# A decoder layer with 32 experts on one core: last two experts' up projections ahead of their down ones, layer norm by channel blocks, parts of block 1 during the first gather, one MB of w_down loaded elsewhere

## The reference

```python
conv_o = silu(layernorm(conv(a * sigmoid(g)) + b_dw, ln_g, ln_b))
h = h + concat([att_o, conv_o]) @ w_out
hn = rmsnorm(h, norm_ffn_g)
gates = top4_softmax(hn @ w_router + b_router)       # (256, 32)
for e in range(32):                                  # w_gu[e]: 1024x2048, w_down[e]: 1024x1024
    hg, hu = split(hn @ w_gu[e] + b_gu[e])
    hg = minimum(hg, 7.0); hu = clip(hu, -7.0, 7.0)
    act = (hu + 1.0) * (hg * sigmoid(1.702 * hg))
    h = h + gates[:, e:e+1] * (act @ w_down[e] + b_down[e])
return rmsnorm(h, norm_final_g)
```

## Time and profile before

| | us |
|---|---|
| median of 3 runs | 1064.13 |
| lowest and highest | 1063.89, 1065.67 |
| the profiled execution | 1063.36 |
| its span in the trace | 1061.6 |
| TensorE busy | 994.2 (94%) |
| VectorE, ScalarE busy | 237.9 (22%), 138.9 (13%) |
| transfers | 421.49 MB, mean 397 GB/s |

### The profile page before, as it was taken

One profiled execution on the slowest core, in us unless ns is written; L12 is line 12 of the kernel. 1 busy time (PEld: TensorE's weight loads), 2 busy tenths in 40 slices (PEclk: granted clock), 3 DMA queues, 4 the chain that ended last, 5 costly groups with the idle time before them and its releaser, 6 DMA issues.

```text
span 1061.6 us, 12949 instructions
## 1 busy us (share of the span) xinstructions
PE 994.2 (94%) x5808; PEld 412.4 (39%) x5809; DVE 237.9 (22%) x531; ACT 138.9 (13%) x264; POOL 14.0 (1%) x27
## 2 busy tenths in 40 slices
PE   9998999999999999999999999999899999889996
PEld 7874443433333333333333333332333333333332
DVE  3995341111111111111111111100111111110113
ACT  4144220101010101010101000100101010100003
POOL 4000000000000000000000000000000000000000
PEclk9999999999999999999999999999999999999999
DMA  9984469999999999999999999999999999999993
GB/s 322 410 357 158 159 254 403 429 427 429 425 429 426 427 427 428 427 428 427 427 428 427 427 426 430 427 428 427 428 427 427 428 427 427 427 428 426 428 427 142
DMA packets 39241, 421.49 MB, mean 397 GB/s; under 512 B 5153, under 2 KB 9297, under 8 KB 14480
## 3 DMA queue, kind: packets, MB, share of 16 engines
q1 hardware_dynamic: 37376, 420.31, 94.5%
q10 hardware_dynamic: 1808, 0.33, 0.2%
HBM read 419.56 MB, written 1.05 MB: 396 GB/s over the span
## 4 chain that ended last, share of the span: by engine, by line
PE 53%; DMA 31%; DVE 12%; ACT 3%; issue 1%; ACTq 0%; DVEq 0%; POOL 0%; POOLq 0%
PE work L965 46%; DMA ring<-in_w_gu 31%; PE resid L965 5%; DVE main L716 4%; DVE main L902 2%; DVE main L899 2%; DVE main L895 2%; PE work L1282 2%; ACT main L585 1%; PE work L1080 0%; PE work L980 0%; ACT ring L528 0%; PE work L1174 0%; DVE main L958 0%; DVE ring L760 0%
## 5 line engine op out<-in xcount | busy, mean ns | idle before, releaser
L965 PE MATMUL work<-ring,main 128*64 128x512 f32 (+1 forms) x3104 | 686.7, 592 | 27.4 <-DMA ring<-in_w_gu 25.1
L965 PEld LDWEIGHTS work<-ring,main 128*64 128x64 f32 (+1 forms) x3104 | 222.8, 138 | 478.1 <-issue 422.2
L895 DVE TENSOR_SCALAR main<-work 128x512 f32<-128x512 f32 x32 | 22.1, 692 | 752.0 <-PE work L965 752.0
L585 ACT ACTIVATE main<-main 128x512 f32<-128x512 f32 x32 | 20.2, 631 | 501.9 <-DVE main L895 501.9
L965 PE MATMUL resid<-main 128*128 128x512 f32 x136 | 71.0, 612 | 0.9 <-DVE main L949 0.9
L965 PE MATMUL work<-ring 128*128 128x256 f32 (+2 forms) x304 | 71.1, 403 | 0.0
L596 ACT ACTIVATE main<-work 64x512 f32<-64x512 f32 x63 | 37.3, 592 | 227.6 <-PE work L965 227.3
L965 PE MATMUL work<-bgu_rows,ident 128*64 128x512 f32 x256 | 62.0, 605 | 0.0
L965 PEld LDWEIGHTS work<-ring 128*128 128x128 f32 (+1 forms) x304 | 54.9, 186 | 13.9 <-issue 6.2
L965 PEld LDWEIGHTS work<-select,main 128*128 128x128 bf16 x1584 | 48.0, 98 | 27.0 <-issue 27.0
L965 PE MATMUL work<-select,main 128*128 128x64 bf16 x1584 | 51.9, 193 | 0.9 <-DVE select L880 0.9
(11 more groups left out here) (178 smaller groups left out, 245.6 us busy)
## 6 DMA issues: line engine op xcount, KB each, us to landing
ring<-in_w_gu SPq DMA_DIRECT2D x128, 2048.0 KB, 40.4
ring<-in_w_down SPq DMA_DIRECT2D x63, 2048.0 KB, 41.3
ring<-in_w_in SPq DMA_DIRECT2D x3, 2048.0 KB, 14.8
ring<-in_w_in SPq DMA_DIRECT2D x4, 1024.0 KB, 12.2
ring<-in_w_out SPq DMA_DIRECT2D x2, 2048.0 KB, 19.5
ring<-in_w_down SPq DMA_DIRECT2D x2, 1024.0 KB, 6.0
main<-in_x SPq DMA_DIRECT2D x2, 512.0 KB, 4.1
result<-main SPq DMA_DIRECT2D x4, 256.0 KB, 2.3
```

Of the source, the lines that this page charges most:

```text
L585: nc.scalar.activation(sig_h, gate_h, ACT.Sigmoid, scale=SWIGLU_ALPHA).then_inc(sig_ready, 1)
L895: V.tensor_scalar(gate_h, work[:, GATE_BANK, :], SWIGLU_LIMIT, None, ALU.min).then_inc(gate_clamped, 1)
L965: return nc.tensor.matmul(out_, lhsT, rhs, start=start, stop=stop, skip_group_check=True)
```

## The change

- `SEQUENCE` sets the order of issue and use: experts 0 to 29 as before, then the up chunks of experts 30 and 31 (180 to 187), then their down chunks (188 to 191). The very last chunk is issued as two halves of 1 MB. TensorE runs expert 31's up projection ahead of expert 30's down projection.
- Layer norm: two additions in pairs in place of the strided sum of squares; each of four channel blocks is scaled by gain and 1/sigma in one operation and has its sigmoid behind it; copy_turned(0) stands ahead of the second products; conv_ready counts blocks, and TensorE's first projection waits for two of four.
- Block 1's parts: one of three operations stays ahead of the choice, one stands behind chosen_b, two third parts behind the first selection. gather_first runs over the parts in its outer loop, and its last of six waits for them. The two warm-up products go; expert 0's bias is split around the place products. turn_gates goes behind expert 3's down projection, b_down is loaded behind expert 2 and used in expert 4 on 32 partitions, with no clearing on GpSimd.
- Chunk 11: its rows 0 and 1 (512 KB each) go to a buffer of their own and to blocks 12 and 13, issued behind chunks 7 and 10; the second half goes to slot 0 as before.
- Final norm: products with the gain by halves ahead of the scale, then scaling; the last half is scaled by ScalarE.
- Some constants (mean_w, dw_cols, others, gates_t) move into other buffers.

```diff
+    SEQUENCE = [(e, i) for e in range(E - 2) for i in range(CHUNKS)]
+    SEQUENCE += [(e, i) for e in (E - 2, E - 1) for i in range(UP_CHUNKS)]
+    SEQUENCE += [(e, i) for e in (E - 2, E - 1) for i in range(UP_CHUNKS, CHUNKS)]
...
+    NUMBER = {chunk_: n for n, chunk_ in enumerate(SEQUENCE)}
...
+    def ups_used(e):
+        return NUMBER[e, UP_CHUNKS - 1] + 1
...
-        return (CHUNKS * e + i) % SLOTS
+        return NUMBER[e, i] % SLOTS
...
+                        CONV_SLOT: ((proj_done, 11), (conv_ready, CB)),
+                        KEYS_SLOT: ((tap_done, CB * OPS), (decay_in, 32), (scores_done, len(GROUPS))),
...
+                src = w_down[e, f:f + 4 * P, :].rearrange("(p h b) n -> p h (b n)", h=2, b=2)
+                to = chunk(slot_of(e, i)).rearrange("p (h n) -> p h n", h=2)
+                sp.dma_start(to[:, 0, :], src[:, 0, :]).then_inc(slot_full[slot_of(e, i)], 16)
+                sp.dma_start(to[:, 1, :], src[:, 1, :]).then_inc(last_half_in, 16)
...
+                sp.dma_start(spare_rows[b], rows_reused()[:, b, :]).then_inc(spare_in, 16)
...
+                sp.wait_ge(first_unit_used, 1)
+                sp.dma_start(unit(0).rearrange("p (b n) -> p b n", b=2), rows_reused()[:, 2:4, :]).then_inc(slot_full[0], 16)
...
+            for number, (e, i) in enumerate(SEQUENCE[:CHUNKS * E]):
+                if number == SLOTS:
+                    load_first_reused()
+                    continue
+                if number >= SLOTS:
+                    sp.wait_ge(slots_used, number - SLOTS + 1)
+                elif number in released:
+                    for used in released[number]:
+                        sp.wait_ge(*used)
+                if (e, i) == (E - 1, CHUNKS - 1):
+                    load_last_in_halves(e, i)
+                else:
                     load_chunk(e, i, slot_of(e, i))
+                if number in (CONV_SLOT, SLOTS - 1):
+                    load_spare_row(0 if number == CONV_SLOT else 1)
...
+                if n == HALVES - 1:
+                    sp.wait_ge(last_ready, 1)
...
-            pool.wait_ge(h_done, 3)
-            nc.gpsimd.memset(bdown_sb, 0.0).then_inc(moe_zeroed, 1)
-            pool.wait_ge(logits_done, TB)
-            nc.gpsimd.memset(gates_t, 0.0).then_inc(moe_zeroed, 1)
...
-            act.wait_ge(normed, 1)
             for c in range(CB):
-                done = nc.scalar.activation(ln_tmp[:, c, :], conv_y[:, c, :], ACT.Sigmoid,
-                                            scale=cols[:, LN_G + c:LN_G + c + 1], bias=cols[:, LN_B + c:LN_B + c + 1])
-            done.then_inc(swish_sig, 1)
+                act.wait_ge(normed, c + 1)
+                nc.scalar.activation(ln_tmp[:, c, :], conv_y[:, c, :], ACT.Sigmoid,
+                                     bias=cols[:, LN_B + c:LN_B + c + 1]).then_inc(swish_sig, 1)
...
+                act.wait_ge(gates_turned, 1)
+                nc.scalar.activation(gates_t, work[0:E, TURN_BANK, 0:SEQ], ACT.Copy).then_inc(gates_t_ready, 1)
...
+                act.wait_ge(slots_used, SLOTS + 1)
+                act.dma_start(bdown_sb, b_down).then_inc(bdown_in, 16)
...
-                if e > 0:
-                    copy_results(e - 1, (e - 1) // 2 % 2, (e - 1) % 2)
-                expert_pass(e)
+                if 0 < e < E - 1:
+                    copy_results(downs_used(e - 1), (e - 1) // 2 % 2, (e - 1) % 2)
+                gate_sigmoid(e)
+                if e < E - 1:
+                    copy_act(e)
                 if e % 2 == 1:
                     copy_scatter(pair, pair % 2, P, (pair - 1) * HALVES if pair > 1 else None)
+                if e == E - 1:
+                    copy_results(downs_used(e - 1), (e - 1) // 2 % 2, (e - 1) % 2)
+                    copy_act(e)
...
             for e in range(E):
                 expert(e)
+                if e == 2:
+                    load_bdown()
+                if e == BDOWN_EXPERT - 1:
+                    copy_gates()
...
+                if t == TB - 1:
+                    act.wait_ge(o_scale, TB)
+                    act.wait_ge(o_gained, HALVES)
+                    nc.scalar.activation(result[:, t, HALF:D], result[:, t, HALF:D], ACT.Copy, scale=stat[:, 10 + t:11 + t])\
+                        .then_inc(last_ready, 1)
...
-            V.tensor_reduce(channel_sum, ln_tmp.rearrange("p c t -> p t c"), AX.X, ALU.add).then_inc(squares_summed, 1)
+            V.tensor_tensor(ln_tmp[:, 0:2, :], ln_tmp[:, 0:2, :], ln_tmp[:, 2:4, :], ALU.add).then_inc(squares_paired, 1)
+            dve.wait_ge(squares_paired, 1)
+            V.tensor_tensor(channel_sum, ln_tmp[:, 0, :], ln_tmp[:, 1, :], ALU.add).then_inc(squares_summed, 1)
...
-            V.tensor_tensor(conv_y, conv_y, ln_s[:, 0, :].unsqueeze(1).to_broadcast([P, CB, SEQ]), ALU.mult)\
-                .then_inc(normed, 1)
             for c in range(CB):
-                if c == 0:
-                    dve.wait_ge(normed, 1)
-                    dve.wait_ge(swish_sig, 1)
-                V.tensor_scalar(conv_y[:, c, :], conv_y[:, c, :], cols[:, LN_G + c:LN_G + c + 1],
-                                cols[:, LN_B + c:LN_B + c + 1], ALU.mult, ALU.add).then_inc(ln_step, 1)
-            dve.wait_ge(ln_step, 1 + CB)
-            V.tensor_tensor(conv_y, conv_y, ln_tmp, ALU.mult).then_inc(conv_ready, 1)
+                V.scalar_tensor_tensor(conv_y[:, c, :], conv_y[:, c, :], cols[:, LN_G + c:LN_G + c + 1], ln_s[:, 0, :],
+                                       ALU.mult, ALU.mult).then_inc(normed, 1)
             copy_turned(0)
+            for c in range(CB):
+                dve.wait_ge(swish_sig, c + 1)
+                V.scalar_tensor_tensor(conv_y[:, c, :], conv_y[:, c, :], cols[:, LN_B + c:LN_B + c + 1], ln_tmp[:, c, :],
+                                       ALU.add, ALU.mult).then_inc(conv_ready, 1)
...
-                third_part(1, halves[1], 6)
+                less_first_part(1, halves[1], 4)
...
-            less_first_part(1, halves[1], 4)
-            third_part(1, halves[0], 5)
             choose()
...
             select_tokens(0, 0, 0)
+            third_part(1, halves[0], 5)
+            third_part(1, halves[1], 6)
             copy_tokens(0)
...
+                half = slice(h * HALF, (h + 1) * HALF)
+                dve.wait_ge(o_squared, 2 * t + h + 1)
+                V.tensor_tensor(result[:, t, half], resid[:, t, half], final_gain[:, half], ALU.mult).then_inc(o_gained, 1)
...
-                inv_rms_of_halves(t, 2 * t, stat[:, 2 * t:2 * t + 1], stat[:, 2 * t + 1:2 * t + 2], stat[:, 4 + t:5 + t],
-                                  (stat[:, 6 + t:7 + t], stat[:, 8 + t:9 + t]), stat[:, 10 + t:11 + t],
-                                  o_squared, o_mean, o_root, o_scale, roots_before=1)
-                for h in range(2):
+                gained(t, 0)
+                V.tensor_scalar(stat[:, 4 + t:5 + t], stat[:, 2 * t:2 * t + 1], 1.0 / D, RMS_EPS, ALU.mult, ALU.add).then_inc(o_mean, 1)
+                dve.wait_ge(o_mean, 2 * t + 1)
+                dve.wait_ge(o_squared, 2 * t + 2)
+                V.tensor_scalar(stat[:, 6 + t:7 + t], stat[:, 2 * t + 1:2 * t + 2], 1.0 / D, stat[:, 4 + t:5 + t], ALU.mult, ALU.add)\
+                    .then_inc(o_mean, 1)
+                gained(t, 1)
+                dve.wait_ge(o_root, t + 2)
+                V.reciprocal(stat[:, 10 + t:11 + t], stat[:, 8 + t:9 + t]).then_inc(o_scale, 1)
+                dve.wait_ge(o_scale, t + 1)
+                for h in range(TB - t):
                     half = slice(h * HALF, (h + 1) * HALF)
-                    V.scalar_tensor_tensor(result[:, t, half], resid[:, t, half], stat[:, 10 + t:11 + t], final_gain[:, half],
-                                           ALU.mult, ALU.mult).then_inc(result_ready, 1)
+                    dve.wait_ge(o_gained, 2 * t + h + 1)
+                    V.tensor_scalar(result[:, t, half], result[:, t, half], stat[:, 10 + t:11 + t], None, ALU.mult).then_inc(result_ready, 1)
...
-            pe.wait_ge(conv_ready, 1)
             arrived("out_conv")
+            pe.wait_ge(conv_ready, 2)
             project("out_conv", 0, 0, range(0, 2))
+            pe.wait_ge(conv_ready, CB)
...
-            keep_warm(2, work[:, GATE_BANK, 0:P])
-            bias(0)
+            bias(0, (GATE_BANK,))
...
+            bias(0, (UP_BANK,))
...
-                    if is_first and kb == KB // 2:
-                        turn_gates()
...
+                    reused = isinstance(n, int) and n == SLOTS // CHUNKS and UP_CHUNKS + m == SLOTS % CHUNKS
+                    if reused:
+                        pe.wait_ge(spare_in, 32)
...
+                        if is_last and f == FB - 2:
+                            pe.wait_ge(last_half_in, 16)
                         lhsT = act_t[:, f % 4, (f // 4) * CAP:(f // 4 + 1) * CAP]
+                        row = w[:, b * D:(b + 1) * D]
+                        if reused:
```

(43 more changed lines are left out.)

111 lines of the change are left out of this document (57 added, 54 removed).

## The result

The changed kernel takes 1057.34 us (median of 4 executions, 1056.44 to 1058.07), the kernel before 1064.90 in the same session (4, 1063.89 to 1065.69): ratio 0.9926, 95% interval 0.9911 to 0.9941. That is 7.6 us less, where 9.4 were forecast. The time lies in the range, and 2.6 above the forecast. The profiled execution took 1057.29, with a span of 1055.6: 6.0 less span than before.

What follows compares the result with a forecast made beforehand. It took the late-starting weight stream as the bound: end = issue of chunk 15 + 176 landings + what follows. Terms summed to -9.4 us from 1063.36, giving 1053.96, forecast as a 1054.7 median; range 1051.5 to 1059.5.

Steps and rivals of the forecast that it cites:

- a: Layer norm by blocks: TensorE's wait for the copy goes, first projection 4.6 us earlier (3.3 to 5.0).
- Rival 4: Layer norm: another wait replaces the copy's, only 1 or 2 of 4.6 us arrive, 1058; chance 0.07.
- b: Choice and first gather: earlier choice and split bias gain 1.1 us, between about 0 and 1.9 depending on clock.
- rival 1: Clock stays at 0.50 through first gather: that stage gains 0, perhaps layer norm 1.3 less; 1055.8 to 1057.1; chance 0.16.
- c: Gate transposes moved from expert 0 to behind expert 3's down projection: 0.4 us less before chunk 15's release.
- d: One MB of chunk 11 issued early: less queue ahead of chunks 12 to 15, gain 1.0 us (0 to 1.9).
- Rival 2: Transfer stream: the early MB pays its full 2.45 us, giving 1053.2; chance 0.10.
- e: b_down's 128 KB moves from the idle stretch into the weight stream: 0.3 us later.
- Rival 5: Weight stream: pace slows with more small rows; if the extra per chunk triples, +13.8 us, 1068.5; chance 0.05.
- f: New order of the last two experts: last down projection ends at 1048.1 in old times, gain 2.8 us (1.5 to 3.1).
- Rival 3: End of kernel: new order pays nothing because the last landing, not the chain, sets the end; 1057.5; chance 0.10.
- g: Final norm with separate gain products and scalings: ends 0.2 us later (-0.3 to +0.9).

Runs made afterwards that it cites:

- e2: Changed kernel with the old layer norm put back (whole-tile product, copy behind the last product): 1060.51 us, ratio 0.9951.
- e3: Changed kernel plus ten small unused products in TensorE's two waits in expert 0: 1054.98 us, ratio 0.9899.
- e1: The changed kernel run once more, unaltered, as base for the other runs: 1055.72 us, ratio 0.9905.
- e4: Changed kernel with the early MB of chunk 11 put back to its old place and time: 1056.39 us, ratio 0.9919.
- e12: The kernel before, with ten small unused products in expert 0's waits and nothing of the change: 1064.79 us, ratio 0.9990.
- e6: Changed kernel with the old choice stage (warm-up products, whole bias, old gather order) put back: 1056.90 us, ratio 0.9926.
- e5: Changed kernel with only the copy of turned probabilities moved back behind the second block products: 1057.86 us, ratio 0.9933.
- e11: Changed kernel plus ten unused products, last activations turned early, and old norm except a split last quarter: 1054.80 us, ratio 0.9906.
- e10: Changed kernel with the last expert's activations turned ahead of the previous expert's down projection, own tile and PSUM bank: 1055.17 us, ratio 0.9908.
- e9: Changed kernel with the stream's last transfer whole (2 MB) instead of two halves: 1057.36 us, ratio 0.9929.
- e7: Changed kernel with the old order of the last two experts and the last transfer whole: 1060.81 us, ratio 0.9965.
- e8: Changed kernel with the old final norm (fused products on VectorE, no ScalarE scaling): 1056.24 us, ratio 0.9919.

## Why the prediction was right, and where not, by its own steps

**a, layer norm: forecast -4.6, measured -5.0** in the profile, at its outer bound, and 5.4 to 5.8 from e2 (97.84) to e3 (92.47) and e1 (92.05). The mechanism is the one that was worked out, the wait of TensorE, and with it the half clock behind it. The copy did come 0.1 sooner, and the second wait was 0.44 instead of 0.6. The Trainium skill (VectorE: DVE Perf Modes, Rules for kernel authors) advises not to fuse chained operations for speed and to keep their number small. The trace doesn't agree for this place: the eight block operations take VectorE 1.67 + 1.67 = 3.34 us, where the six before took 1.23 + 1.38 + 1.23 = 3.84, and TensorE's wait of 3.80 is gone. Rival 4 fell.

**b, choice and first gather: forecast -1.1, measured +0.1** in the profile (-5.0 becomes -4.9). This is rival 1, its first half: 0.50 through bias, gather and on to 138. It isn't always so. From the first projection to the first expert it is 47.47 in the profile of the changed kernel, and 45.18 in e3 and e4, where the clock was full; in the kernel before 47.33 with its half-clock stretch, and 46.73 with full clock there (e12), of which 0.34 is the half clock at the start of the first projection. So the edit is worth 46.73 - 0.34 - 45.18 = 1.2 at full clock, inside the bounds of 0 and 1.9, and e6 shows nothing of it in the medians. The Trainium skill (TensorE: Matmul & The Clock Gate, What's actually happening) has it that the throttled clock is the default and activity releases it, from which the prediction worked out a term of 0. In both profiles of the changed kernel the term is near 0, but the traces don't bear that reason out: the clock fell while TensorE was busy without a break, it fell in e6 with the warm-up products too, and in e3 and e4 the same work ran at full clock.

**c, gates later: forecast -0.4, measured -0.45** (144.42 to 158.78 is 14.36, 139.52 to 153.41 is 13.89).

**The step that was missing: +1.7.** The clock at 158 to 162 us. The prediction followed the clock up to the first gather only, and handed the shift on "whole" to chunk 15. Expert 0's down projection at 8.78 instead of 7.09 keeps the slot for chunk 15 that much longer: issued 3.6 earlier, not 6.1. In the kernel before the same wait of TensorE stood there and the down projection took 7.09. In the changed kernel and the experiments on it that gave TensorE nothing to do there, it took 8.78 to 10.05 in nine profiles of ten (7.09 in e5), and with the products 7.09 in both (e3, e11; e12 says little, as the kernel before had 7.09 without them). What the stretch costs is shown by e5: 1.3 to 1.5 at chunk 183. That products in the wait remove it there fits two profiles, but the half clock then stood elsewhere, in e3 at 184 us and in e11 at 882, and of the 1.6 that they win at the issue of chunk 15, 0 and 1.0 to 1.3 reach the end of the stream. In the medians no gain is clear: 0.7 against e1 in the same session, 2.0 against all nine executions of the changed kernel, 0.9 in the kernel before. A limit shows here that the prediction's "end = issue of chunk 15 + 176 landings" lacks: with chunk 14 landing at 162.9 in e3 as in e10, chunk 15, issued 1.6 earlier, still landed at 169.2.

**d, early MB: forecast -1.0, measured -0.35** (what is left of -4.0 at chunk 16 after the terms above), and 0.4 by e4 at chunk 17 against e9 and e10. The remainder isn't firm: e1, with the same two issue times, has chunk 16 at 176.2 instead of 177.9. Rival 2 (2.45) fell. The landing of chunk 15 did shrink by the full 2.0, to the 7.8 of an empty queue, and by e4 some 1.2 of that is the early MB's: the step took a landing for a gain, where the chunks behind it show how little of it stays.

**e, b_down: forecast +0.3, measured +0.1:** chunk 183, the last that TensorE waits for, lands 4.0 earlier (1006.04 and 1002.07), as chunk 16 did. This holds the pace of the stream too, and 128 KB can't be told apart in it: from chunk 17 to chunk 190 it takes 853.5 before and 853.8 changed, 853.7 to 854.6 in the other runs but e3, which has 855.3, and 854.3 in e12, which has nothing of the change. Rival 5 fell.

**f, last two experts: forecast -2.8, measured -2.6** in the profile (-6.5 less the stream's -3.96 at chunk 183), 2.85 by e7 against e1, 3.8 in e7's median. One step in it was wrong without harm: the last up projection doesn't wait for its transfers, as TensorE itself is the bound there (its 64 products are one row of 13.90 from 1012.31 on, and the down projection of 30 follows at once). The last half lands at 1041.4 and is wanted at 1037.33 + 0.75 x 7.09 = 1042.65; 1.2 were free, as forecast. Rival 3 fell.

**g, final norm: forecast +0.2, measured +0.54,** inside its bounds; of it 0.04 is computing, as e8 shows with the same length, and 0.5 the last write, which differs by as much between profiles of one and the same norm (2.9 to 3.4).

**Sum:** -5.0 + 0.1 - 0.45 + 1.7 - 0.35 + 0.1 - 2.6 + 0.54 = -6.0, as in the spans. To the forecast's -9.4 that is 3.4: b 1.2, the clock behind it 1.7, d 0.65, f 0.2, g 0.35, and 0.6 the other way in a and e. So the clock theory carries 2.9 of it, and the other theory 1.2, most of that in d. This is the account of one profile against one profile. The bounds of the forecast's terms add up to -12.3 and -4.0, not to -12.4 and -4.4. How near the median comes to the forecast is in part luck: it lies 2.6 above it in the first session and 1.0 in the next (1055.72). The medians lie further apart than the profiles (7.6 against 6.1), as the profiled execution of the kernel before was 1.5 faster than that kernel's median of 1064.90.

What stays open: where the lead of chunk 15 goes in e3; why the clock falls at the choice in some executions of the same work and not in others (half there in the profiles of the changed kernel, e1, e5, e6 and e7, full in e2 to e4 and e8 to e11); and whether the early turning pays 1.2 if it stands between the two chunks of the down projection of expert 30, behind VectorE's last product and still ahead of its use. That wasn't tried.

## What to carry to other kernels

A stream that has to become gapless is delayed by waits of TensorE long before it, so such a wait is removed by asking what the releasing engine does ahead of the operation waited for: here a shorter chain ahead of the copy brought 3.9 us and the copy's place in the queue 1.1. When shifts are handed on through a chain of TensorE work, follow the granted clock along the whole chain up to the moment that counts, and list as places where it may fall each wait on the way, and here the router's small products as well. A few useless products in one wait took the half clock from that place in both profiles, but it stood elsewhere then, and a gain in the medians isn't shown: hold such a fix against a run with the same clock ahead of it, up to the last landing, and not against the first number that moves. Add up the terms with the next limit in mind: a transfer issued earlier still lands behind the one ahead of it. A gain at a handover between two stages is no larger than the wait that the moved step meets at its new place: look up when its input is ready there.

## What the runs showed of the hardware that was not expected

Matmuls of one form at the two clocks: four bias products 1.08 and 1.98 us, the first gather's 48 small ones 1.57 to 1.61, and 2.27 to 2.55 where the clock was half for part of them. The place of the half-clock stretch moves by itself: the work up to 132 us is the same in the changed kernel, e3 and e4, and granted 0.50, 1.00 and 1.00 there. Executions of the changed kernel spread over 4.2 us (1053.80 to 1057.99 in one session), those of e3 and e11, with the ten products, over 1.0 and 1.6. The mean granted clock of every execution is on record and goes with it: 0.997 and 0.998 for the three fastest of e1 (1053.80 to 1055.72), 0.994 and 0.992 for the two slowest. A mean below 0.995 stands in 22 of 55 executions of the changed kernel and of the runs without products on it (e2, e4 to e10), and in none of the nine of e3 and e11. That the clock makes the spread fits this; where it fell in an unprofiled execution isn't on record.

The last write of 256 KB took 2.4 to 3.8 us from the end of the last result to the end of the span, with the same instructions, in e11 the longest: 2.4 to 2.5 in both profiles of the kernel before, 2.9 to 3.4 in eleven of the changed kernel's kind. Half a microsecond won in the final norm can't be seen beside it.
